# Reordering the vector and scalar work around the first feed-forward block of a two-layer streaming encoder, and GpSimd's accumulating loads in its two-pair groups

## The reference, cut to what matters

```python
x = x + 0.5 * swiglu(rms_norm(x, g_norm[l, 0]), w_ffn_gate[l, 0], w_ffn_up[l, 0], w_ffn_down[l, 0])
h = rms_norm(x, g_norm[l, 1])
... attention on h, added to x ...
x = x + 0.5 * swiglu(rms_norm(x, g_norm[l, 2]), w_ffn_gate[l, 1], w_ffn_up[l, 1], w_ffn_down[l, 1])

def swiglu(x, w_gate, w_up, w_down):
    return (jax.nn.silu(x @ w_gate) * (x @ w_up)) @ w_down
```

## Time and profile before

| | us |
|---|---|
| three runs | 2455.98, 2460.01, 2460.65 |
| median of them | 2460.01 |
| the profiled execution, its own time | 2457.78 |
| its span, first to last instruction | 2455.7 |
| PE busy with matmuls | 2402.1 (98% of the span) |
| DVE, ACT, POOL busy | 1858.7, 1336.1, 544.4 |

### The profile page before, as it was taken

The page is one execution under the profiler, slowest core; times in us unless marked ns, Lnnn a source line. Parts: engine busy times, 40 slices in busy tenths (PEclk is TensorE's granted clock), DMA queues, the critical chain, the costliest instruction groups (busy, mean ns, idle before and its releaser), DMA issues. The chain is left out here.

```text
span 2455.7 us, 48881 instructions
## 1 busy us (share of the span) xinstructions
PE 2402.1 (98%) x18377; PEld 2261.9 (92%) x18377; DVE 1858.7 (76%) x3709; ACT 1336.1 (54%) x2873; POOL 544.4 (22%) x422
## 2 busy tenths in 40 slices
PE   9899999999999999999999999999999999999998
PEld 9899999888778999999988999999996699999998
DVE  7887979422787888787925889787928878887865
ACT  6555656201785655555622655555618856555554
POOL 1222222354000121222135222222131002222210
PEclk9999999999999999999999999999999999999999
DMA  5557575333863465756523775766467544766642
GB/s 146 121 116 144 106 148 101 95 116 97 304 237 94 97 140 103 144 115 140 104 79 127 187 143 115 139 127 126 107 227 265 209 112 94 145 125 126 139 101 82
DMA packets 423237, 334.20 MB, mean 136 GB/s; under 512 B 20641, under 2 KB 383834, under 8 KB 423010
## 3 DMA queue, kind: packets, MB, share of 16 engines
q1 hardware_dynamic: 281296, 246.98, 32.2%
q0 software_dynamic: 133136, 65.82, 21.9%
q10 hardware_dynamic: 8578, 18.37, 2.1%
HBM read 314.98 MB, written 16.13 MB: 135 GB/s over the span
## 5 line engine op out<-in xcount | busy, mean ns | idle before, releaser
L997 PE MATMUL PS<-x_area,w_area 128*128 128x320 f32 x3096 | 483.1, 310 | 2.3 <-ACT PS L1804 2.3
L997 PEld LDWEIGHTS PS<-x_area,w_area 128*128 128x128 f32 x3096 | 461.6, 188 | 2.7 <-ACT PS L1804 2.6
L1718 ACT ACTIVATE w_area<-R 128x512 fp32r<-128x512 f32 (+2 forms) x583 | 325.5, 567 | 204.9 <-DVE R L2414 92.3
L2393 DVE TENSOR_TENSOR w_area<-R,w_area 128x512 fp32r<-128x512 f32 (+2 forms) x583 | 357.7, 615 | 87.1 <-ACT w_area L1718 86.5
L2393 DVE TENSOR_TENSOR r_area<-R,r_area 128x512 fp32r<-128x512 f32 (+2 forms) x437 | 265.8, 617 | 94.4 <-ACT r_area L1718 88.8
L1804 ACT ACTIVATE PS<-PS 128x320 f32<-128x320 f32 x438 | 178.3, 416 | 215.6 <-PE PS L997 189.9
L997 PE MATMUL PS<-r_area,w_area 128*128 128x320 f32 x1584 | 266.4, 311 | 10.7 <-ACT PS L1804 6.2
L1718 ACT ACTIVATE r_area<-R 128x512 fp32r<-128x512 f32 (+2 forms) x437 | 247.7, 567 | 47.2 <-DVE R L2414 20.2
L997 PEld LDWEIGHTS PS<-r_area,w_area 128*128 128x128 f32 x1584 | 239.1, 188 | 18.3 <-ACT PS L1804 11.2
L1226 PE MATMUL PS<-w_area,xn_hi 128*128 128x512 f32 x800 | 251.5, 396 | 0.5 <-DVE xT L2578 0.3
L997 PE MATMUL PS<-r_area 128*128 128x320 f32 x1392 | 236.5, 311 | 2.2 <-DVE r_area L2648 1.8
(11 more groups left out here) (348 smaller groups left out, 4152.6 us busy)
## 6 DMA issues: line engine op xcount, KB each, us to landing
R<-in_w_ffn_up_dram SPq DMA_DIRECT2D x45, 512.0 KB, 5.2
R<-in_w_ffn_gate_dram SPq DMA_DIRECT2D x43, 512.0 KB, 5.1
R<-in_w_ffn_up_dram SPq DMA_DIRECT2D x86, 256.0 KB, 4.1
R<-in_w_ffn_up_dram POOLq DMA_DIRECT2D x86, 256.0 KB, 4.8
R<-in_w_ffn_gate_dram SPq DMA_DIRECT2D x82, 256.0 KB, 4.6
R<-in_w_ffn_gate_dram POOLq DMA_DIRECT2D x81, 256.0 KB, 5.5
R<-in_w_ffn_down_dram SPq DMA_DIRECT2D x52, 384.0 KB, 3.9
R<-in_w_ffn_down_dram SPq DMA_DIRECT2D x88, 192.0 KB, 3.7
```

Source lines behind the costliest of these rows:

```text
L997: last = pe.matmul(PS[:, bank, 0:HT], a[:, k, :], b, start=(start and opens), stop=(k == n - 1 and a is lo), skip_group_check=True)
L1718: act.activation(role_parts(f, g, s, role)[0], role_source(f, g, s, role), ACT.Copy).then_inc(sem("early_cast") if key in EARLY_COUNT else ...
L2393: dve.tensor_tensor(lo, role_source(f, g, s, role), hi.bitcast(F32), ALU.subtract).then_inc(sem("early_split") if key in EARLY_COUNT else ...
```

## The change

Two things. (a) In the input loop and behind it the operands of the first FFN are made in another order: parts of "5" from k = 1, the first parts of "y" and "7" inside the loop, "6" and "4" of DVE earlier. In set n == 1 of the first FFN ACT makes the second copy and `copy_fifth` ahead of the previous set's silu. The hook behind set n == 1 is gone; the first pair's parts "2", "7" and "4" are made inside `opening_down` (the new argument `left`), behind the second pair's "1"; `FIRST_HIDDEN` numbers the parts in the new order. (b) In POOL's order, for the last two down sets of a group of two pairs (sets 6 and 7 of group 0, in all four FFNs) the third sum is issued ahead of the first sum that stood before it. In the diff lines without a change are mostly left out.

```diff
@@ -64,6 +64,7 @@
 HIDDEN_PARTS = ("1", "5", "7", "2", "4")
+FIRST_HIDDEN = ((0, "1"), (0, "5"), (1, "1"), (0, "2"), (0, "7"), (1, "5"), (0, "4"), (1, "7"), (1, "2"), (1, "4"))
@@ -249,6 +250,8 @@
                 self.hidden.update({(f, g, k, x): len(self.hidden) + n + 1 for n, x in enumerate(parts)})
+            if (f, g) == (0, 0):
+                self.hidden.update({(f, g, k, x): n + 1 for n, (k, x) in enumerate(FIRST_HIDDEN)})
             if (f, g) in PLAIN:
@@ -272,10 +275,11 @@
     blocks = [("x", k) for k in range(KB)]
-    near = [("5", k) for k in range(4)]
+    near, far = ([(x, k) for k in range(4)] for x in "5y")
     opening = (by_operand("5764"),
-               blocks[:6] + near[0:1] + blocks[6:7] + near[1:2] + blocks[7:] + near[2:3] + by_operand("y") + near[3:] + by_operand("674"),
-               blocks[:6] + near[0:1] + blocks[6:7] + near[1:2] + blocks[7:] + near[2:] + by_operand("674"))
+               blocks[:2] + near[0:1] + blocks[2:3] + near[1:2] + blocks[3:6] + near[2:3] + far[0:1] + blocks[6:7] + near[3:] + far[1:2] + blocks[7:]
+               + far[2:] + by_operand("674"),
+               blocks[:2] + near[0:1] + blocks[2:3] + near[1:2] + blocks[3:6] + near[2:3] + blocks[6:7] + near[3:] + blocks[7:] + by_operand("674"))
     late = (by_operand("5764"), by_operand("5y764123"), by_operand("5761243"))
@@ -875,8 +879,12 @@
                     first_sum(at)
+                ahead = [at for at in order[1:] if is_down(*at) and GROUPS[at[0]] == 2 and at[1] >= width(at[0]) + DOWN_SETS - 2]
                 for n, at in enumerate(order):
-                    third_sum(at)
+                    if at not in ahead:
+                        third_sum(at)
+                    if n + 1 < len(order) and order[n + 1] in ahead:
+                        third_sum(order[n + 1])
                     if n + 2 < len(order):
@@ -1857,13 +1865,17 @@
-            def opening_down(f, prev, cur, then):
+            def opening_down(f, prev, cur, then, left=None):
...
                 hidden_rows(f, *prev, "1")
+                if left is not None:
+                    left("27")
                 copy_rows(f, *cur, 1)
...
                 hidden_rows(f, *prev, "5")
+                if left is not None:
+                    left("4")
                 hidden_rows(f, *prev, "7")
@@ -1881,7 +1893,7 @@
                     if opens_down(*cur):
-                        opening_down(f, prev, cur, then)
+                        opening_down(f, prev, cur, then, after_set["left"] if (f, n) == (0, 2) else None)
                         continue
@@ -1896,6 +1908,9 @@
                     role_high(f, *cur, "S4")
+                    if n == 1 and f == 0:
+                        copy_rows(f, *cur, 2)
+                        copy_fifth(f, *cur)
                     if n:
@@ -1904,7 +1919,7 @@
                         square(event, unsquared.pop())
-                    if n == 1:
+                    if n == 1 and f > 0:
                         copy_rows(f, *cur, 2)
@@ -2182,8 +2197,10 @@
                 x_high(0, 0, "x", k)
+                if k in (1, 2, 5, 6):
+                    x_high(0, 0, "5", k - 1 if k < 3 else k - 3)
                 if k >= 5:
-                    x_high(0, 0, "5", k - 5)
+                    x_high(0, 0, "y", k - 5)
                 if k == 0:
@@ -2218,14 +2235,14 @@
-            x_highs("y")
+            x_high(0, 0, "y", 3)
             role_high(0, 0, 1, "W21")
             role_high(0, 0, 1, "W22")
-            x_high(0, 0, "5", 3)
+            first_roles(0, 0, ("W11",))
             root(PS[:, 6:8, 0:HT])
...
             first_silu(1)
-            first_roles(0, 0, ("W11", "S1"))
+            first_roles(0, 0, ("S1",))
             x_highs("6")
@@ -2239,7 +2256,7 @@
             ffn(0, None, partial(finish_tile, 0, 0, 0, 1), "qkv",
-                {n: partial(first_hidden_casts, parts) for n, parts in enumerate(("57", "24"))}, 0)
+                {0: partial(first_hidden_casts, "5"), "left": first_hidden_casts}, 0)
             act.wait_ge(w_used, BASE["qkv"])
@@ -2665,13 +2682,21 @@
-            def opening_down(f, prev, cur, then):
-
-                role_sum(f, *cur, "S4")
+            def opening_down(f, prev, cur, then, left=None):
+
+                if left is None:
+                    role_sum(f, *cur, "S4")
                 hidden_lows(f, *prev, "1")
+                if left is not None:
+                    left[0]()
+                    role_sum(f, *cur, "S4")
                 sums_out(f, *prev)
+                if left is not None:
+                    left[1]()
                 hidden_sums(f, *prev, ("5", "7", "6"))
                 hidden_lows(f, *prev, "5")
+                if left is not None:
+                    left[2]()
                 role_low(f, *then, "W11")
@@ -3117,10 +3142,12 @@
                 dve.wait_ge(sem("x_evac_act"), k + 1)
-                if k >= 5:
-                    x_sum(0, 0, "5", k - 5)
+                if k in (1, 2, 4, 5):
+                    x_sum(0, 0, "5", k - 1 if k < 3 else k - 2)
+                if k in (2, 3, 6, 7):
+                    x_low(0, 0, "5", k - 2 if k < 4 else k - 4)
                 if k >= 6:
-                    x_low(0, 0, "5", k - 6)
+                    x_sum(0, 0, "7", k - 6)
                 block_low(k)
@@ -3146,7 +3173,7 @@
-            x_sum(0, 0, "5", 3)
+            x_sum(0, 0, "7", 2)
             dve.wait_ge(sem("x_squared"), ACT_SQUARES)
@@ -3169,21 +3196,19 @@
-            x_sums("7")
+            x_sum(0, 0, "7", 3)
+            x_sums("6")
             role_low(0, 0, 1, "W21")
-            role_low(0, 0, 1, "W22")
             first_gate(0)
             first_gate(1)
-            x_sums("6")
-            for k in range(2, 4):
-                x_low(0, 0, "5", k)
+            role_low(0, 0, 1, "W22")
+            x_sums("4")
             role_low(0, 0, 2, "W11")
...
             first_hidden(0)
-            x_sums("4")
             role_low(0, 0, 2, "S2")
@@ -3206,12 +3231,12 @@
                 first_hidden_sums("4")
-                hidden_parts_low(0, 0, 0, "7", None)
                 hidden_parts_low(0, 0, 0, "2", halves(tt[:, 3, :]))
-                hidden_parts_low(0, 0, 0, "4", None)
                 dve.wait_ge(sem("act_ready"), PLAN.hidden[0, 0, 0, "2"])
-            ffn(0, 1, 0, 0, 1, "qkv", {0: first_hidden_near, 1: first_hidden_far}, partial(x_lows, "4"))
+            first_hidden_left = (first_hidden_far, partial(hidden_parts_low, 0, 0, 0, "7", None),
+                                 partial(hidden_parts_low, 0, 0, 0, "4", None))
+            ffn(0, 1, 0, 0, 1, "qkv", {0: first_hidden_near, "left": first_hidden_left}, partial(x_lows, "4"))
```

## The result

| | before | after |
|---|---|---|
| median of 15 runs each, us | 2460.31 | 2473.59 |
| their spread | 2454.35 to 2465.94 | 2465.23 to 2479.61 |
| ratio, 95% interval | | 1.0054 (1.0045 to 1.0063) |
| the profiled execution, its own time and span | 2457.78, 2455.7 | 2472.37, 2470.3 |

The changed kernel is slower, by 0.54% or 13.3 us. Between the two profiled executions the difference is 14.6 us. In the kernel after, the product's line 997 is 1005, the operand copy's 1804 is 1812, the casts' 1718 is 1726, the low halves' 2393 is 2410, the hidden low parts' 2648 is 2665, the role sums' 2414 is 2431, and POOL's 864 and 873 are 868 and 877.

The account below looks back on a forecast made before the run. With PE 98% busy, DVE's list of work was taken as the true bound between the first pair and the opening set. Input loop +0.1, shorter list -2.8, part (b) +0.6: -2.1 from 2458.9 gives 2456.8 us, range 2451.8 to 2461.2.

Parts of the forecast that it names:

- This product comes at about 79.7: Opening down set, first FFN: S3 of (0,4) starts at about 79.7 us, as DVE's list is 2.8 us shorter.
- the sum had 2.7: Part (a) in the total: +0.1 us for the input loop and -2.8 us for DVE's shorter list behind it.
- about 2.4 us ahead of S2: Opening down set: a new PE gap of about 2.4 us, released by DVE's hidden low part (L2648).
- about 1.3: Opening down set: a second new PE gap of about 1.3 us ahead of the last pair's S1, released by L2648.
- the wait of 1.52 ahead of S3 of (0,5): First FFN: PE's 1.52 us wait for a third sum's landing moves along with DVE's S2 sum and stays.
- The rival that the opening set swallows the gain through the clock: Opening set: clock falls to 1.2 GHz in the new gaps, costing about 1.7 us; 2458.6 us, chance 0.17.
- +0.15 a place: Part (b), set 7: PE's S3 follows the later landing as before; +0.15 us, applied to six places.
- +0.6 in all: Part (b) total: 0.9 us for six places, less 0.3 swallowed by ACT's later waits; bounds -4.5 and +7.
- The term for set 6, +0.1 a place: Set 6, second FFN: third sum starts unchanged, first sum of set 7 later, ACT's copy 0.1 us later.
- +7 (each place 0.9 later): Upper bound of part (b), sets 6 and 7 in all FFNs: 0.9 us later at each place, +7 us.
- The rival *Slower: Sets 6 and 7: late first sums delay ACT's S1 cast and copy and DVE's list; 2463.2 us, chance 0.08.
- the sign given for a wrong part (b): Other three FFNs: PE's waits for ACT's copies in group 0 gone, or over 0.5 us longer each.

Follow-up runs that it names:

- e1: Kernel before with part (a) only, POOL's old order kept; 2456.21 us against 2459.25, ratio 0.9986.
- e2: Kernel before with part (b) only, POOL's new order; 2473.94 us, ratio 1.0049 to the kernel before.
- e12: Changed kernel with SP's 512 KB far load of (1,0) held until that set's first sum has landed; 2465.83 us, ratio 1.003 to the kernel before.
- e6: Kernel before, POOL's order kept, but first sums of set 7 and (1,0) wait for the DVE sum the third sums wait for; 2465.63 us, ratio 1.0021.
- e5: Changed kernel, sets 6 and 7 of group 0: ACT's copy ahead of the next S1 cast, DVE's S3 low half ahead of the next S2 sum; 2462.95 us.
- e8: Changed kernel with eight extra small matmuls on PE ahead of the wait in set 7 of group 0; 2469.85 us, ratio 1.0037 to the kernel before.
- e9: Kernel before plus part (a), ACT's copy before next S1 cast in sets 6 and 7, DVE's S3 low half before S2 sum in set 7; 2454.41 us.
- e4: Kernel before with part (b) for set 7 alone; ratio 1.0021 to the kernel before.

## Why the prediction was wrong

The prediction was 2456.8 us, in a range of 2451.8 to 2461.2, and the kernel took 2473.59.

**Part (a) was right.** "This product comes at about 79.7": S3 of (0,4) came at 80.1, 2.4 us ahead of before, and S3 of (0,5) 2.84 us ahead; alone the part gave 3.4 us where the sum had 2.7. The new gap of "about 2.4 us ahead of S2" measured 2.48. The one of "about 1.3" ahead of the last pair's S1 was 0.52, and the wait of 1.52 ahead of S3 of (0,5) did not stay but shrank to 1.01, with DVE's low half as the releaser. So S3 of (0,4) came 0.4 us later than I had it, and the shorter wait behind it gave 0.5 back. The rival that the opening set swallows the gain through the clock did not come. The granted clock does fall behind the new gap (0.59 from 76 to 78 us), but S3 of (0,5) is still 2.84 us ahead, and in e1, where the clock does not fall there (1.00 from 74 to 80 us), it is 3.21 us ahead: the fall costs some 0.4 us here, and the kernel before has one too, at 74 us.

**Part (b) failed, at one term of the sum.** I wrote that the first sum of (1,0) "starts 2.2 us later and lands about where the third one did, at 890.3 or somewhat after", and took +0.15 a place and +0.6 in all. It measured +12 (e2), 3 us for each FFN. The term for set 6, +0.1 a place, failed as well: set 6 alone measured 1.0023, some 5.7 us, and set 7 alone 1.0021, some 5.2. Three things were wrong in it:

- *The start.* The first sum was put behind an instruction that waits for DVE, the same wait that holds back the third sum. It then went out among SP's loads for the next set, about 1 MB in 2.2 us. The slot that it had used, ahead of those loads, was left unused (DMA engines 1% busy in the 1.2 us before them). So I moved a transfer and kept the duration that it had in its old place, 3.6 to 5.2 us; in its new one it took 7.5. e12 shows this by taking one load away. From the third sum's issue, which DVE sets, to the last landing of the pair, set 7 took 6.0 to 6.3 us before and 7.6 to 8.7 after in the four FFNs.
- *What stands behind the landing.* I noted DVE's 0.69 us sum between that landing and S3's low half, and ACT's cast ahead of the copy, and treated them as an exchange: one waits for the first sum in the place of the third. But in the old order the early lander fed the S2 sum while the late one was under way; in the new one the S2 sum, the S3 low half behind it and the S1 cast with the copy behind that all start at the last landing. e6 against e2 puts the order, slower transfer included, at more than half of the 12, and e5 shows both lists at it.
- *The clock.* I priced its fall as a rival of part (a), not in part (b). It fell behind the wait of set 7 in three of the four FFNs, at about 1.4 us each (12 matmuls in 3.32 instead of 1.92); e8 got back 3.7.

The bound of "+7 (each place 0.9 later)" was too low for the same reasons: it took its 0.9 from a third sum's 5.0 us of transit among other loads, and 6.2 us stood two lines below. The trace before even has nearly the same case, 256 KB issued straight behind another sum and among SP's loads: the third sum of (1,0), issued at 892.15:

```profile
DMA to landing us min/median/max: 8.3/8.3/8.3
```

The range therefore left out the true case. The rival *Slower* had the right place, mechanism and releaser, a chance of 0.08, and a price of 7 us for part (b) where e2 measured 12. The rule quoted beside it, from the Trainium skill's "DMA: Bandwidth & Descriptors" (Queues, rings and completion order), is that on each DMA engine descriptors are taken in ring order; the Trainium skill says it there of the queues of SP and ACT, and adds that completion is not first in, first out for an issuing engine. For POOL's queue the trace after agrees with the order: of each of the eight pairs the sum issued second landed second. The rule quoted in part (b), from the Trainium skill's "DMA: Bandwidth & Descriptors" (Anatomy of one DMA), gives an estimate of some 2.6 us for 256 KB; the trace does not agree, with 7.5 us beside SP's loads.

**The rest.** In set 7 of the second FFN the third sum was issued at 888.53 instead of 884.05, 4.5 us later, with PE 5.0 us later: 0.5 us nearer to PE, where I had written within 0.3. The first sum of (1,0) was issued 6.2 us later, 1.2 against PE, where I had written about 2. The waits of set 7 grew by over 0.5 us each, which was the sign given for a wrong part (b).

**One part of the difference is likely not the change's.** In the second FFN of the profile after, PE waited 2.23 us at set 5:

```profile
881.74 1.84 PE L1005 MATMUL PS<-r_area,w_area 128*128 128x320 f32 x6 [2.23 <-ACT PS L1812]
```

The change does not touch set 5. Its third sum took 5.5 us to land where it took 3.9 before. The same gap stands in e9, whose POOL order is that of the kernel before and whose third sum took 5.7 there, and not in e6, e8 or e12:

```profile
878.36 1.97 PE L1001 MATMUL PS<-r_area,w_area 128*128 128x320 f32 x6 [2.40 <-ACT PS L1808]
```

It is worth 2.8 us in this profile, clock included. That it comes and goes between executions of one kernel is the likely reading; it is not shown, since each kernel has one profile. That is why I go by the ratios and not by one profile's difference.

**What stays open.** How the 12 us part between lateness (5 by e6) and the rest, and how that rest parts between the slower transfer and the lists; and why the transit of set 5's third sum varies.

## What to carry to other kernels

A transfer moved to another place in a queue must be priced by what else is under way at its new issue time, and by the slot that it leaves idle, not by the duration that it had. Where two engines' ordered lists wait for a pair of landings, the question is not only when each lands but what stands behind the last one. That the transfer which feeds the longer list should land first is the likely reading here; no run turned the order round with both transfers as quick as before. And a longer wait of PE can cost more than its length: in three of four places here the clock fell behind it.

## What the runs showed of the hardware

The same accumulating load of 256 KB, the first sum of (1,0) in the second FFN, took 4.8, 5.2, 6.2, 7.5 and 7.7 us from issue to landing in e6, the kernel before, e12, the changed kernel and e5, with the DMA engines 69, 75, 85, 92 and 91% busy in that time. The share alone does not set it: e4 has 6.5 us at 97%. An issue on POOL's queue straight behind another took 1.75 and 1.82 us in the rows above, in the place of 1.19 to 1.28. With e8's small matmuls ahead of the wait the granted clock stayed at 1.00 in the second FFN, where it had fallen to 0.66. The length of a wait alone did not decide it: it fell behind one of 2.09 us in the second FFN and not behind one of 2.24 in the third.
